# Closing a channel group behind the first block of the next, in the token mixer of a hybrid decoder step

## The reference

```python
u = xn @ w_in                                   # 1024 -> 8 groups of 10 blocks of 128 columns, dt apart
a = glu_v * sigmoid(glu_g)
a = causal_dwconv(concat([conf_buf, a]), conf_dw_w, conf_dw_b)       # 31 taps
xbc = silu(causal_dwconv(concat([ssm_buf, xbc]), ssm_conv_w, ssm_conv_b))   # 4 taps
xs, bm, cm = split(xbc)
dt = softplus(dt_raw + dt_bias); A = -exp(a_log)
# per chunk of 128 tokens (16 meta tokens first, each running sequence by itself)
w = (cm @ bm.T)[..., None] * decay * dt
y = w @ xs + (cm @ h) * exp(cum)
h = exp(cum[-1]) * h + (tail * bm) @ xs          # tail = exp(cum[-1] - cum) * dt
y = (y + d_skip * xs) * silu(z)
y = y * rsqrt(mean(y * y, over the 256 channels of the group) + EPS) * ssm_norm_w
```

## Time and profile before

| | us |
|---|---|
| median of 3 runs | 1691.87 (1690.29 to 1692.17) |
| the profiled execution | 1683.87 |
| its span | 1681.9 |
| TensorE busy | 1403.0 (83%) |
| VectorE busy | 1284.3 (76%) |
| ScalarE busy | 765.5 (46%) |
| GpSimd busy | 335.7 (20%) |

### The profile page before, as it was taken

The page is one execution under the profiler, slowest core; times in us unless marked ns, Lnnn a source line. Parts: engine busy times, 40 slices in busy tenths (PEclk is TensorE's granted clock), DMA queues, the critical chain, the costliest instruction groups (busy, mean ns, idle before and its releaser), DMA issues. The chain is left out here.

```text
span 1681.9 us, 26627 instructions
## 1 busy us (share of the span) xinstructions
PE 1403.0 (83%) x8709; PEld 1242.7 (74%) x8709; DVE 1284.3 (76%) x2063; ACT 765.5 (46%) x1189; POOL 335.7 (20%) x382
## 2 busy tenths in 40 slices
PE   2899989899898998989893999997078998998980
PEld 2898887888888898887892899975067777777760
DVE  4148989989898898989987445533469999999974
ACT  3135253343534335243342333312058888888861
POOL 0123322333123233222220000000301111111112
PEclk9599998999989899898996999998579999999995
DMA  4142341714316252252533724403188999998936
GB/s 142 26 120 71 91 132 51 191 44 134 101 41 189 60 156 70 76 148 62 167 82 128 235 64 149 135 26 122 67 327 324 344 334 331 346 337 336 340 129 224
DMA packets 191349, 271.40 MB, mean 161 GB/s; under 512 B 15884, under 2 KB 154358, under 8 KB 174886
## 3 DMA queue, kind: packets, MB, share of 16 engines
q1 hardware_dynamic: 178350, 245.62, 45.1%
q0 software_dynamic: 9968, 18.25, 3.1%
q10 hardware_dynamic: 2992, 7.03, 1.1%
HBM read 237.95 MB, written 50.26 MB: 171 GB/s over the span
## 5 line engine op out<-in xcount | busy, mean ns | idle before, releaser
L759 PE MATMUL pu<-xh,wh 128*128 128x304 f32 (+1 forms) x1280 | 290.1, 310 | 46.0 <-DVE wl L233 39.3
L759 PE MATMUL pu<-xl,wh 128*128 128x304 f32 (+1 forms) x1280 | 281.1, 302 | 0.0
L759 PE MATMUL pu<-xh,wl 128*128 128x304 f32 (+1 forms) x1280 | 279.3, 301 | 0.0
L759 PEld LDWEIGHTS pu<-xh,wh 128*128 128x128 f32 x1280 | 207.6, 200 | 51.9 <-DVE wl L233 41.1
L759 PEld LDWEIGHTS pu<-xl,wh 128*128 128x128 f32 x1280 | 209.6, 200 | 0.0
L759 PEld LDWEIGHTS pu<-xh,wl 128*128 128x128 f32 x1280 | 207.1, 199 | 0.0
L233 POOL TENSOR_TENSOR wl<-ring,wh 128x1024 fp32r<-128x1024 f32 x48 | 119.7, 2494 | 356.3 <-ACT wh L502 354.3
L886 DVE SCALAR_TENSOR_TENSOR cacc<-a_p,gc,cacc 128x528 f32<-128x528 f32 x232 | 189.7, 818 | 0.0
L1998 DVE TENSOR_TENSOR W13l<-W,W13h 128x1024 fp32r<-128x1024 f32 x160 | 184.8, 1216 | 5.0 <-ACT W13h L1950 4.8
L502 ACT ACTIVATE wh<-ring 128x1024 fp32r<-128x1024 f32 x80 | 84.3, 1055 | 192.8 <-PE pu L759 191.4
L1909 PE MATMUL eh<-W13h,xch 128*128 128x512 f32 x320 | 131.0, 409 | 43.4 <-DVE xcl L1998 39.1
(11 more groups left out here) (392 smaller groups left out, 2858.9 us busy)
## 6 DMA issues: line engine op xcount, KB each, us to landing
W<-in_exp_w SPq DMA_DIRECT2D x120, 1024.0 KB, 8.2
ring<-in_w_in SPq DMA_DIRECT2D x80, 512.0 KB, 4.1
stage<-decay_rows SPq DMA_DIRECT2D x8, 1120.0 KB, 7.1
x<-in_state_ssm SPq DMA_DIRECT2D x16, 512.0 KB, 7.0
out_new_ssm_sample<-x SPq DMA_DIRECT2D x16, 512.0 KB, 8.3
wraw<-in_ssm_out_w SPq DMA_DIRECT2D x8, 1024.0 KB, 9.7
Ed<-decay_rows SPq DMA_DIRECT2D x32, 140.0 KB, 7.3
gates<-gbuf ACTq DMA_DIRECT2D x16, 280.0 KB, 2.1
```

The costliest lines, as they stand in the source:

```text
L759: last = pe.matmul(u_cols(r, a, b), w[:, k % RING, j, :], x[:, j, a:b], start=(j == 0 and n == 0), stop=(j == KD - 1 and n == 2))
```

## The change

- `low` of all ten blocks goes to VectorE; the splits of the next group's blocks 0 and 1 stand ahead of `stage2(5)` and behind the states.
- `closing(g)` (on TensorE: the wait for the states, transposes, sums; on ScalarE: the copies of the output rows and the roots) moves behind `block(0)` or `raw(0)` of the next group. The sums go to `turn` (the PSUM tiles of the chunks) and not to `pu`: `U_TILES = 10`. ScalarE's `gate(1)` comes behind the square.
- On VectorE the reciprocal and `yout` (`scaled`) and the last 14 taps (`TRAIL = 14`) move between the SSD convolutions of the next group.
- The fourth SSD tap with the bias is a ScalarE Identity with scale and bias from the product itself; VectorE adds three taps to it.
- `xdt` is written by ScalarE: four copies of 64 columns with dt as scale; `Tt` keeps only B and C B, one copy of 256 columns. `xtl` on GpSimd is `xdt` times a tail without dt.
- The 32 sample columns are no longer done tap by tap: one product over overlapping windows (`seen`) and one reduction, for the 31 taps (32 x 31 elements) and for the four SSD rows (4 x 32 x 4, steps of 8 elements, since `raw_s` is laid out token first). Their SiLU is done for four rows at once.
- SyncE stores `aconv` (`conv_out`) behind blocks 8 and 9 of the next group. The groups 0 and G - 1 are written out apart from the loop.

```diff
@@ low_done
+            eng.wait_ge(s_wld, BLOCKS * g + k + 1)
@@ ScalarE
+            def closing(g):
+                act.wait_ge(s_out, 2 * g + 2)
...
+                act.activation(pk_rows[:, :, :].rearrange("r q c -> r (q c)"), pC[0:27, :], ACT.Copy).then_inc(s_outev, 1)
...
+                for r in range(2):
+                    act.wait_ge(s_sum, 2 * g + r + 1)
+                    act.activation(zc[:, 0, 280 * r:280 * r + 280], turn[r][:, 0:280], ACT.Sqrt,
+                                   scale=1.0 / (2 * P), bias=eps[:, :]).then_inc(s_root, 1)
...
+                    act.activation(raw_p[:, q, SK - 1:], u_cols(q, SAMP, T), ACT.Copy)
+                    r = R_X + 5 * q
+                    act.activation(cv[:, q, SAMP:T], u_cols(q, SAMP, T), ACT.Identity, scale=gc[:, r + SK - 1:r + SK],
+                                   bias=gc[:, r + SK:r + SK + 1]).then_inc(s_raw, 1)
...
                 raw(0)
+                if not is_first:
+                    closing(g - 1)
                 raw(1)
+                silu(0)
                 raw(2)
-                silu(0)
+                silu(1)
                 raw(3)
-                silu(1)
                 silu(2)
+                silu(3)
+                silu_s()
...
+                    for h in range(HG):
+                        act.activation(xdt[0:S, j % 2, h, :], src[0:S, HD * h:HD * h + HD], ACT.Copy,
+                                       scale=gdt[0:S, ci, h:h + 1])
...
-                gate(1)
                 act.wait_ge(s_yz, g + 1)
                 act.activation(th[:, :, :], ybuf[:, :, :], ACT.Square).then_inc(s_sq2, 1)
+                gate(1)
@@ TensorE
+                block(0)
+                if not is_first:
+                    closing(g - 1)
+                for k in range(1, 6):
                     block(k)
@@ VectorE
+            def conf_samples(g):
...
+                    seen = bass.AP(src.tensor, src.offset, [src.ap[0], [n, NSAMP], [1, TSAMP], [1, CK]])
...
+                    k.link(dve.tensor_tensor(prod.rearrange("p (b t j) -> p b t j", b=NSAMP, t=TSAMP), seen, w, ALU.mult))
+                    k.link(dve.tensor_reduce(csum[:, :], prod.rearrange("p (s j) -> p s j", j=CK), AX_X, ALU.add))
...
+                trail(4)
+                split(g, 2)
+                dve.wait_ge(s_gc, 3 * g + 3)
                 dve.wait_ge(s_y, 6 * g + 1)
+                ssm_conv(0)
+                trail(2)
+                if not is_first:
+                    scaled(g - 1)
+                silu(0)
+                split(g, 3)
+                ssm_conv(1)
+                if not is_first:
+                    conf_samples(g - 1)
+                trail(2)
+                silu(1)
+                split(g, 4)
+                ssm_conv(2)
+                trail(3)
+                silu(2)
+                split(g, 5)
+                ssm_conv(3)
+                ssm_samples()
+                trail(3)
                 silu(3)
+                silu_s()
+                split(g, 6)
...
                 for j in range(5):
-                    taps(1)
+                    taps(2)
                     stage2(j)
...
-                taps(8)
+                taps(4)
+                if not is_last:
+                    split(g + 1, 0)
                 stage2(5)
```

More of the change, by code:

```diff
@@ L359, in _ @@
             results_out(G - 1)
+            conv_out(G - 1)
             sp.wait_ge(s_wraw, 32)
@@ L740, in _, with closing, group @@
             pe.wait_ge(s_dect, 4)
-            with pe.Fori(0, G) as g:
+            def closing(g):
+                pe.wait_ge(s_y, 6 * g + 6 + 1)
+                pe.wait_ge(s_pk, 7 * g + 7 + 1)
+                for q in range(4):
+                    last = pe.transpose(pC[0:27, P * q:P * q + P], pk[:, q, :], ident[:, :])
+                last.then_inc(s_out, 1)
+                for i in range(2):
+                    pe.transpose(pY[:, P * i:P * i + P], hT[:, 2 * i:2 * i + 2, :].rearrange("n h p -> n (h p)"), ident[:, :])
+                pe.transpose(pY[0:62, 2 * P:3 * P], pa[:, :], ident[:, :]).then_inc(s_out, 1)
+                pe.wait_ge(s_sq2, g + 1)
+                pe.wait_ge(s_hnew, 4 * g + 4 + 1)
+                for r in range(2):
+                    for i in range(2):
+                        last = pe.matmul(turn[r][:, 0:280], ones[:, :], th[:, i, 280 * r:280 * r + 280],
+                                         start=(i == 0), stop=(i == 1))
+                    last.then_inc(s_sum, 1)
+            def group(g, is_first=False):
                 U0 = U_TILES * g
@@ L1075, in _ @@
                 dve.wait_ge(s_ga, 2 * g + 2)
-                split(7)
-                tap = iter(range(CK))
-                def taps(n):
-                    for _ in range(n):
-                        conf_tap(next(tap))
+                split(g, 7)
                 taps(3)
@@ L1111, in _ @@
                     last.then_inc(s_hnew, 1)
-                taps(4)
-                dve.wait_ge(s_ufree, U_TILES * g + 12 + 1)
-                dve.reciprocal(zc[:, 1, :], zc[:, 0, :]).then_inc(s_rec, 1)
-                dve.wait_ge(s_rec, g + 1)
-                dve.wait_ge(s_yst, 16 * g + 1)
-                for i in range(2):
-                    stt(yout[:, i, :], ybuf[:, i, :], gc[:, R_NW + i:R_NW + i + 1], zc[:, 1, :],
-                        ALU.mult, ALU.mult).then_inc(s_yn, 1)
-                taps(11)
-                assert next(tap, None) is None
-                k.leave(G)
+                if not is_last:
+                    split(g + 1, 1)
+                assert next(ahead, None) is None
+            group(0, is_first=True)
+            with dve.Fori(0, G - 2) as g1:
+                k.enter(g1, DVE_STEPS)
+                group(g1 + 1)
+                k.leave(G - 2)
+            group(G - 1, is_last=True)
+            scaled(G - 1)
+            conf_samples(G - 1)
+            conf_taps(G - 1, range(CK - TRAIL, CK))
 OT = [(0, SAMP)] + CHUNKS[2:]
```

266 lines of the change are left out of this document (136 added, 130 removed).

## The result

The changed kernel takes 1667.79 us (median of four runs, 1666.85 to 1668.5), the kernel before beside it 1691.08 (four runs, 1686.64 to 1692.17). The ratio is 0.9862, with a 95% interval of 0.9839 to 0.9884: 23 us less, where 28 were forecast.

A forecast was written before the change was run, and what follows sets the result against it. VectorE was taken to bound each group's first half, mostly TensorE the second. Groups of 97.8 against 102.0 us save 29 over seven; group 0 gains 1, the end loses 2: 28 off 1691.87 gives 1664, range 1640 to 1682.

The forecast's parts named there:

- first half: End of the state matmuls to block 6, set by VectorE's chain: 46.1 us a group against 48.1.
- the sum: Inner group 97.8 against 102.0 us, seven times 29 in all; group 0 gains about 1, the end loses 2: 28.
- the doubling that I assumed: SSD sample product's 32-byte step doubling its time: first half 0.65 us longer, forecast 4.5 us higher; left out of the sum.
- Second half: From block 6 on, mostly set by TensorE: 53.8 - 1.8 - 1.1 + 0.8 = 51.7 us a group.
- so the 1.8 us of slow matmuls go: Block 6: waits of about 2 us let TensorE's clock hold, saving 1.8 us a group.
- (c): Rival: TensorE's clock falls after shorter waits too: at block 6 1677 us (0.15), also at chunk 2 1689 (0.05).
- The end: After the last group nothing hides the closing: 22.8 us behind the last state matmul, before 20.9; 2 lost.
- (a): The forecast as summed: 1664 us, within 1650 to 1678; chance 0.50.
- (b): Rival: TensorE alone sets the first half, VectorE's chain at least 4 us shorter; 93 a group, 1633 us; chance 0.20.
- (d): Rival: ScalarE's longer rows make the chunk chain bound the second half; at 1.3 us more a chunk 1708 us; chance 0.10.
- (e): Rival: splits on GpSimd cost VectorE nothing and the change only loads it; excluded by the rows, given no chance.

The follow-up runs named there:

- the run shows 3: Changed kernel with the SSD sample product reading elements 4 bytes apart in place of 32, right sample sums left out: one execution, 1664.79 us.
- The run with all orders: Also the last version: changed kernel, 8 taps ahead of split 2, first SiLU's Tanh before `raw(1)`, chunk 1's output before its taps, five end taps before the reciprocal: 1628.6 us.
- the GpSimd run: Changed kernel with the low parts of blocks 2 to 5 given back to GpSimd, everything else as in it: 1693.53 us.

## Why the prediction was right, and by how much its terms were off

**The mechanism held in the first half, and for the second it had the clock wrong.** VectorE's load, the split wait and its place, the taps under 0.8 us, the reductions of 1.2, no wait for `hT` in chunks 3 to 5 and the hold of 2.1 us by GpSimd's splits came as forecast. The first half fell from 48.3 to 46.3 in the mean, by the 2.0 of the sum; the second from 53.4 to 52.8, by 0.6 and not 2.1. Three of the signs that it named failed: VectorE stood still 1.2 us and not 4 ahead of the first SiLU (its 4.0 lie ahead of split 2), only three of seven groups are 98 apart, and TensorE at 1.2 GHz in block 6, a sign of being wrong, is there in four of seven.

**First half: 46.1 forecast.** From the start of block 0 (which is the end of the state matmuls) to block 6 it is 322.50 - 275.65 = 46.85 here and 45.05 to 47.1 over seven groups, 46.3 in the mean. Inside, two terms were off and cancelled, which was luck. The first SiLU was to start at 21.4 and did, at 297.06 - 275.65 = 21.41. But block 0 ran slowly for 8 pairs, 1.7 us, which the prediction didn't have (before, it began behind the closing and at the full clock), and the closing took 2.4 us and not 4.9: I took its duration from a stretch at the lower clock, and behind block 0 it runs at the full one. In the two groups whose block 0 is fast the SiLU starts at 19.6. The wait before it was 1.2 and not 3.8, since split 2 came at 9.4 and not 7.4 and the taps and roots behind it as much later. (In this half VectorE waited some 6 us for others. The prediction's text says 4.9, but its own terms, 2.0 ahead of split 2 and 3.8, make 5.8.) Behind the SiLU come 25.4 us of own work against 24.7: 0.47 of the 0.7 is the product of 512 elements, at 1.12 and not 0.65. TensorE's waits are 1.65, none and 2.55 for 1.7, 0.3 and 2.1, 4.2 in all for 4.0.

The Trainium skill's rule quoted in the prediction (page "SBUF — State Buffer", section "Door 1: The DMA port swizzle", a penalty for each access to a new 16-byte line) bears out here: 1.12 us at a step of 32 bytes, 0.686 at 4. The page gives no size; with the doubling that I assumed, the sum was 4.5 us higher than mine, and the run shows 3.

**Second half: 51.7 forecast.** Measured 51.4 to 54.0, 52.7 in the mean. The wait at chunk 2 was to become 0.8 and is 1.2. Its cause was ScalarE's four copies only in part: with the two taps behind chunk 1's output the wait was gone from chunk 2, so VectorE's taps were in its chain. The run with `xdt` back on VectorE (0.9) doesn't part the two, since it lengthens VectorE's work by what it takes off ScalarE's. The four small copies are 0.9 and the copy of 256 columns 0.4, against 1.05 and 0.35. The step that failed is "so the 1.8 us of slow matmuls go": the first pair of block 6 is fast (0.53), yet in four of the seven groups TensorE falls to the lower clock two to five pairs later:

```profile
323.64 0.42 PE L794 MATMUL pu<-xl,wh 128*128 128x304 f32 x2
323.89 0.56 PE L794 MATMUL pu<-xh,wl 128*128 128x304 f32 x2
324.25 0.67 PE L794 MATMUL pu<-xh,wh 128*128 128x304 f32 x2
```

Every group has two or three such stretches of 6 to 11 pairs, 17 to 23 pairs in all; the kernel before has 17 to 20. The slow pairs moved, and they didn't go. Block 6's stretch alone doesn't make a group long: two of the three groups of 98.0 have it too. What those three share is that the state matmuls at their start run at the full clock (4.5 us up to block 0, and 5.4 to 5.8 in the other four). Rival (c) came in part: it gave 13 us for a slow start of block 6 everywhere; four groups of seven times 1.5 are 6. (The kernel before has one more wait between 1.1 and 5.25 us than (c) says, 1.60 at 177.37.) And the sum took 53.8 for each second half of the kernel before, while the last of its seven was 50.7, as it has no next group's split on GpSimd: 3 us that weren't there to be gained.

**The end: 2 forecast, 4.9 measured.** From the last group's first state matmul to VectorE's first instruction behind the mixer it is 34.0 us, before 29.2. The last reciprocal and the last tap of the changed kernel:

```profile
875.22 3.65 DVE L1033 RECIPROCAL zc<-zc 128x560 f32<-128x560 f32 x1 [3.96 <-ACT zc L542]
...
893.51 0.76 DVE L914 SCALAR_TENSOR_TENSOR aout<-a_p,gc,cacc 128x528 f32<-128x528 f32 x1
```

14 taps stand behind a wait of 4.0 that could have covered five of them. The run with all orders did that: 28.9 us for the same stretch.

**The sum.** In the profiled executions: seven groups 21.0 (29 forecast), all ahead of them 1.9 (1), the end -4.9 (-2): 18 us up to the end of the mixer. Spans differ by 15.9, the untouched part behind the mixer having lost 2. The medians differ by 23, since the profiled execution of before was among its fastest (1683.87 in 1683.2 to 1698.5). Trace against trace, then, the change gave 16 us where the sum had 28; that the median of 1667.79 came within 4 us of 1664 owes 8 us to taking the 28 off the median, and that is luck too. It lies in (a)'s own range.

**The rivals.** (b), TensorE alone, is what the reorders came to: 93 a group in (b), 92.3 to 95.2 in the last version, 1628.6 for its far end of 1633 (1631 by its own terms, 62 less the 2 of the end). (d) is out: no chunk waited for ScalarE's longer rows beyond chunk 2. (e) was rightly excluded; the rows of the GpSimd run show the hold directly.

**What stays open.** Why TensorE's clock holds through some groups and not through their twins. Undoing single parts cost 9, 15, 19 and 26 us, together three times the gain; only of the 15 does most, 12 us, follow from the part undone, of the 26 some 12, and of the 9 some 4.5. What the title names, the closing moved behind block 0, and with it the reciprocal and the 14 taps and the sums outside `pu`, was never undone by itself, nor were the SSD sample sums. The trace shows that TensorE's closing takes 2.4 us in its new place for 4.9 in the old, and that block 0 now runs in part at the lower clock in five of seven groups; what the move is worth in all is not shown.

## What to carry to other kernels

A helper engine's price is how long it holds up the busy one: a GpSimd split under a busy VectorE cost it 2.1 us, against 1.1 for doing it itself; alone, in the kernel before, taking the splits off it bought nothing, as the wait went to another block. Before you move a late stage behind the next early one, list for each engine what now stands ahead of its first wait; the independent work (here taps) belongs there, and this was worth more (39 us) than the change (23). Measure from mark to mark (here block 0, block 6, the next block 0) and find the engine that sets each stretch: a wait of the other engine can stay the same while the stretch grows. And compare groups within one trace by their granted clock before you give a difference between two kernels to the edit.

## What the runs showed of the hardware that was not expected

TensorE's granted clock made 7.5 us of 102 between two groups of the same work in one execution (94.61 us at 0.98, 102.09 at 0.90). Small matmuls strewn among large ones brought the clock down 3 us into the mixed stretch and held it down for about 20 us; the same small ones in a row cost 1.7 to 2.3 us behind them. VectorE's taps, products and SiLUs that began behind the start of a GpSimd split were held up; a reciprocal from 296.72 kept its 3.65 us beside a split from 299.13, in the GpSimd run, but no row has one that began behind a split. A product of 512 elements with a step of 32 bytes took 1.12 us in place of 0.69, while a product of 992 elements over overlapping windows in a row took 1.19, where a plain one of 1024 takes 1.22. A reduction of 992 elements took 1.19 and one of 512 0.69, the same as the products of their size.
